# Router logits from the residual with scaled weights, and the tokens copied out by halves of the chunks

## The reference

```python
h = rmsnorm(x, lw['norm_ffn']) * (1 + scale2) + shift2
x = x + gate2 * moe_ffn(h, lw)

def moe_ffn(h, lw):
    scores = jax.nn.sigmoid((x @ lw['router_w']).astype(jnp.float32))   # x is h here, 256 tokens x 1024
    sel = scores + lw['router_bias'].astype(jnp.float32)
    ...                                    # the best 4 of 8 groups, in them the best 6 of 64 experts
    gates = gates / jnp.sum(gates, axis=-1, keepdims=True) * ROUTED_SCALE
    routed = moe_dispatch(x, eidx, gates, lw['exp_w_gate'], lw['exp_w_up'], lw['exp_w_down'])
    shared = swiglu(x, lw['sh_w_gate'], lw['sh_w_up'], lw['sh_w_down'])
    return (routed + shared).reshape(B, L, D)
```

## Time and profile before

| | us |
|---|---|
| median of 3 runs | 1344.55 |
| lowest and highest | 1344.04 and 1345.78 |
| the profiled execution, its own time | 1345.73 |
| its span | 1343.9 |
| mean granted TensorE clock | 0.967 |

### The profile page before, as it was taken

One profiled execution on the slowest core, in us unless ns is written; L12 is line 12 of the kernel. 1 busy time (PEld: TensorE's weight loads), 2 busy tenths in 40 slices (PEclk: granted clock), 3 DMA queues, 4 the chain that ended last, 5 costly groups with the idle time before them and its releaser, 6 DMA issues.

```text
span 1343.9 us, 22748 instructions
## 1 busy us (share of the span) xinstructions
PE 1235.8 (92%) x9612; PEld 838.9 (62%) x9612; DVE 273.3 (20%) x714; ACT 236.1 (18%) x521; POOL 2.8 (0%) x13
## 2 busy tenths in 40 slices
PE   6999999999998889888999999999999889888986
PEld 4566687667755566556565668866767565556554
DVE  1253342110111010101034424411011010101012
ACT  2363131110010001000134431311010001000102
POOL 0000000000000000000000000000000000000000
PEclk8999999999999899889999999999999899899989
DMA  9879849999999999999956663999999999999992
GB/s 385 323 316 346 348 190 410 383 422 420 420 420 422 422 422 422 422 422 422 402 201 264 244 242 152 415 383 422 422 420 421 421 421 422 422 422 422 422 419 85
DMA packets 80657, 496.58 MB, mean 369 GB/s; under 512 B 10576, under 2 KB 12880, under 8 KB 24784
## 3 DMA queue, kind: packets, MB, share of 16 engines
q1 hardware_dynamic: 76528, 493.63, 89.7%
q10 hardware_dynamic: 4064, 2.00, 0.5%
HBM read 493.60 MB, written 2.00 MB: 369 GB/s over the span
## 4 chain that ended last, share of the span: by engine, by line
PE 71%; DMA 23%; DVE 2%; issue 1%; SPq 1%; ACT 1%; DVEq 0%; ACTq 0%
DMA dn<-in_exp_w_down 19%; PE PS L2147 15%; PE PS L2183 13%; PE PS L2077 8%; PE PS L2084 7%; PE PS L1649 7%; PE PS L1981 4%; DMA gu<-in_exp_w_gate 3%; PE PS L1573 2%; PE PS L2043 2%; PE PS L1605 2%; DMA gu<-in_w_in 1%; PE PS L1772 1%; PE PS L1783 1%; PE PS L2123 1%
## 5 line engine op out<-in xcount | busy, mean ns | idle before, releaser
L2147 PE MATMUL PS<-gu,arena 128*32 128x256 f32 (+1 forms) x3072 | 316.6, 381 | 0.0
L2183 PE MATMUL PS<-arena 128*64 128x512 f32 (+1 forms) x336 | 177.9, 679 | 62.1 <-DMA dn<-in_exp_w_down 60.6
L2147 PEld LDWEIGHTS PS<-gu,arena 128*32 128x32 f32 (+1 forms) x3072 | 183.9, 118 | 79.0 <-issue 18.0
L2183 PE MATMUL PS<-dn,arena 128*32 128x512 f32 (+1 forms) x688 | 185.6, 637 | 0.0
L2077 PE MATMUL PS<-arena 128*128 128x128 f32 x1408 | 176.3, 278 | 0.5 <-ACT arena L1023 0.5
L2077 PEld LDWEIGHTS PS<-arena 128*128 128x128 f32 x1408 | 164.1, 192 | 17.9 <-issue 16.7
L2084 PE MATMUL PS<-arena 128*128 128x256 f32 x704 | 160.2, 380 | 1.4 <-ACT arena L1006 1.4
L2147 PE MATMUL PS<-arena 128*64 128x256 f32 (+1 forms) x672 | 152.0, 379 | 0.0
L2084 PEld LDWEIGHTS PS<-arena 128*128 128x128 f32 x704 | 130.2, 190 | 20.5 <-ACT arena L1006 3.2
L1484 DVE TENSOR_TENSOR arena<-arena,PS 128x256 f32<-128x256 f32 x44 | 18.5, 422 | 563.7 <-ACT arena L1019 563.7
L1006 ACT ACTIVATE arena<-PS 128x512 f32<-128x512 f32 x88 | 52.6, 597 | 459.0 <-PE PS L2183 459.0
(11 more groups left out here) (257 smaller groups left out, 1022.9 us busy)
## 6 DMA issues: line engine op xcount, KB each, us to landing
gu<-in_exp_w_gate SPq DMA_DIRECT2D x106, 1024.0 KB, 16.5
gu<-in_exp_w_up SPq DMA_DIRECT2D x86, 1024.0 KB, 17.6
dn<-in_exp_w_down SPq DMA_DIRECT2D x86, 1024.0 KB, 18.1
arena<-in_exp_w_up SPq DMA_DIRECT2D x42, 1024.0 KB, 14.9
arena<-in_exp_w_down SPq DMA_DIRECT2D x42, 1024.0 KB, 16.7
gu<-in_w_ada SPq DMA_DIRECT2D x20, 2048.0 KB, 8.8
xh<-in_exp_w_gate SPq DMA_DIRECT2D x22, 1024.0 KB, 11.3
gu<-in_w_in SPq DMA_DIRECT2D x8, 2048.0 KB, 13.1
```

The source lines that it names most:

```text
L2147: ins = mmul(PS[w * h:w * h + w, 5, FF * half:FF * half + FF], xg[:, k, w * h:w * h + w], weights[half][:, k], start=(k == 0), stop=(k == ...
L2183: ins = mmul(PS[w * h:w * h + w, 7 - n, :], hidT[:, j * P + w * h:j * P + w * h + w], weights[:, j, 512 * n:512 * n + 512], start=(j == 0) ...
```

## The change

The logits are no longer taken from `hT`. Since h = x * r * amp + shift, with r the inverse root of a token, `amp` and `shift` a number for each channel and group, the logits are r * (x @ (amp * W)) + shift @ W. So the product x @ (amp * W) can run on `xT` before r is there.

- **Weights.** In the last projection VectorE makes `scaled_rt` (two products 128x512, one for each group), `shift_rt` (two more) and `shift_sum` (the sum of `shift_rt` over the chunks). They wait for `router_in`. `amplify` for this norm moves from the end of the squares to before the copy of `kdec`.
- **TensorE in the norm.** The fills are gone. In their place stand one product that sums `shift_sum` over the partitions into bank 2 and the 16 products of the router, 8 before the sum of squares, 4 after it, 4 after the spread.
- **VectorE.** It copies the shift's logits out of bank 2, norms four chunks and modulates group 1 of three (`SECOND_D`), makes the logits (two instructions 128x64), and norms the other four.
- **ScalarE.** The table of the sigmoid is loaded by a 1-element call ahead of the first modulation. ScalarE modulates group 0 of chunks 0 to 2, takes the sigmoid of the logits, modulates both groups of chunks 3 to 5, copies out the tokens of chunks 0 to 3 (`tokens_out(l, 0)`), modulates chunks 6 and 7, and copies out chunks 4 to 7.
- **TensorE behind the norm.** It takes chunk by chunk: the two transposes, the shared gate's first half (chunks 0 to 6) and, for chunks 0 to 3, its second half. What was four products between `tallied` and `ranked` is one. The list of experts goes to bank 1 instead of 2.
- `h_d` counts fewer steps (`h_d_count`), also in SP's wait ahead of line 693. In layer 0's first norm a semaphore between two VectorE steps is replaced by another, and TensorE waits for the later of the two.

```diff
+        SECOND_D = 3
...
-                    A(hT[:, c, 0:P], xn[:, c, 0:P], ACT.Identity, scale=amp[:, w, c, 0:1],
-                      bias=mod[:, l, 3 * w, c, 0:1]).then_inc(S["h_a"], 1)
+                    for g in range(2 if k % 2 and c >= SECOND_D else 1):
+                        ins = A(hT[:, c, g * P:g * P + P], xn[:, c, g * P:g * P + P], ACT.Identity, scale=amp[:, w, c, g:g + 1],
+                                bias=mod[:, l, 3 * w, c, g:g + 1])
+                    ins.then_inc(S["h_a"], 1)
+                    if k % 2 and c == SECOND_D - 1:
+                        act.wait_ge(S["logits_ready"], l + 1)
+                        A(score, score, ACT.Sigmoid).then_inc(S["sig_exp"], 1)
+                    if k % 2 and c == 5:
+                        tokens_out(l, 0)
...
+                if k % 2:
+
+                    normed(0)
+                    for c in range(SECOND_D):
+                        normed(c + 1)
+                        modulated(c)
+                    v.wait_ge(S["router_done"], l + 1)
+                    for g in range(G):
+                        ins = stt(score[:, g], PS[:, 4, g * E:g * E + E], small[:, G + g:G + g + 1],
+                                  shift_sum[:, g * E:g * E + E], ALU.mult, ALU.add)
+                    ins.then_inc(S["logits_ready"], 1)
+                    for c in range(SECOND_D + 1, NC_):
+                        normed(c)
+                    return
...
+                def routed(cs):
+                    for c in cs:
+                        pe.wait_ge(S["x_bank"], x_steps(2 * l) + [c in step for step in STEPS[0]].index(True) + 1)
+                        for g in range(G):
+                            ins = mmul(PS[:, 4, g * E:g * E + E], xT[:, c, g * P:g * P + P], scaled_rt[:, g, c],
+                                       start=(c == 0 and g == 0), stop=(c == NC_ - 1), skip_group_check=True)
+                    return ins
+                pe.wait_ge(S["x_bank"], x_steps(2 * l) + 1)
+                pe.wait_ge(S["router_scaled"], l + 1)
+                mmul(PS[:, 2, 0:G * E], C("ones"), shift_sum, start=True, stop=True)
+                routed(range(4))
```

More of the change, by code:

```diff
@@ L810, in ada, with tokens_out @@
                 settle("ada_r")
+            def tokens_out(l, half):
+                act.wait_ge(S["t_h"], 2 * l + half + 1)
+                A(h_tok[:, :, 4 * half:4 * half + 4], PS[:, 2 * half:2 * half + 2, :].rearrange("p g (c t) -> p g c t", c=4), ACT.Copy
+                  ).then_inc(S["h_tok_a"], 1)
             def norm(k):
@@ L1349, in _ @@
                 ada(ADA_BY[l] - 1)
+                amplify(2 * l + 1)
                 v.wait_ge(S["t_k"], l + 1)
@@ L1354, in _ @@
                 v.tensor_copy(dk_tok, PS[:, 2, 256:512]).then_inc(S["ktok_ready"], 1)
+                v.wait_ge(S["router_in"], 16 * (l + 1))
+                router = w_rt.rearrange("p (c e) -> p c e", c=NC_)
+                for g in range(G):
+                    tt(scaled_rt[:, g], router, bc(amp[:, 1, :, g], 2, E), ALU.mult)
+                tt(shift_rt[:, 0], router, bc(mod[:, l, 3, :, 0], 2, E), ALU.mult)
                 v.wait_ge(S["t_mix"], 2 * l + 2)
@@ L1385, in _ @@
                         add_squares(STEPS[0][b - 1])
-                amplify(2 * l + 1)
                 add_squares(STEPS[0][-1], True)
@@ L1633, in norm @@
                 ins.then_inc(S["ss_ready"], 1)
-                fill(1)
-                pe.wait_ge(S["rstd_ready"], k // 2 + 1)
+                routed(range(4, 6))
+                pe.wait_ge(S["rstd_ready"], l + 1)
                 for g in range(G):
@@ L1640, in norm @@
                 ins.then_inc(S["rstd_spread"], 1)
-                fill(2)
+                routed(range(6, NC_)).then_inc(S["router_done"], 1)
             def project(bank, o, lhs, rhs, fresh=None):
@@ L2023, in _, with shared_part @@
                 norm(2 * l + 1)
[L2026 to L2046 removed]
+                w = piece(("shared", l, 0)).rearrange("p (u k t j) -> p u k j t", u=2, k=NC_, j=2)
+                def shared_part(bank, u, j, ks, first=None):
+                    for k in ks:
+                        ins = mmul(PS[:, bank, j * T:j * T + T], w[:, u, k, j], hT[:, k, :],
+                                   start=(k == 0 if first is None else first), stop=(k == NC_ - 1), skip_group_check=True)
+                    return ins
+                for c in range(NC_):
+                    pe.wait_ge(S["h_a"], NC_ * (2 * l + 1) + c + 1)
+                    pe.wait_ge(S["h_d"], h_d_count(2 * l + 1, c))
+                    for g in range(G):
+                        ins = turn(PS[:, 2 * (c // 4) + g, (c % 4) * P:(c % 4) * P + P], hT[:, c, g * P:g * P + P])
+                    if c % 4 == 3:
+                        ins.then_inc(S["t_h"], 1)
+                    if c < NC_ - 1:
+                        shared_part(6, 0, 0, (c,), first=(c == 0))
+                    if c < 4:
+                        shared_part(6, 0, 1, (c,), first=False)
                 pe.wait_ge(S["routed"], l + 1)
```

71 lines of the change are left out of this document (32 added, 39 removed).

## The result

The changed kernel takes 1338.29 us (median of 5; 1336.17 to 1340.38) where the kernel before, measured beside it, takes 1345.34 (median of 5): a ratio of 0.9949 [0.9936, 0.9963], 7.05 us faster. The forecast of 1340.2 with a range from 1339.0 to 1343.3 had the direction right, and the mechanism as far as TensorE's lead goes.

What follows compares the result with a forecast made beforehand. TensorE's work sets the first expert round, and its lead pays up to the transfer holes, 3.7 us in layer 0 and 2.0 in layer 1. Gains of 2.4 and 2.0 sum to 4.4: 1344.55 to 1340.2 us, range 1339.0 to 1343.3.

Steps and rivals of the forecast that it cites:

- Weights in the last projection, 0 us: VectorE's weight products and sum around the mixT copy: hidden in idle time, costing 0 us.
- Router in place of the fills, 0.3 us lost at the spread: TensorE in the norm: router records at 0.127 us each start the spread 0.3 us later, bounds 0 and 0.4.
- Logits and routing, 2.1 to 2.2 us earlier: VectorE in the norm: logits between the norms let the routing start 2.1 to 2.2 us earlier.
- ScalarE: ScalarE in the norm: table load fits by 0.2 us, modulations take 0.4 each, the count starts at most 1.1 late.
- TensorE 2.4 us ahead, bounds 1.5 and 2.7: TensorE behind the norm: list of experts and first expert round come 2.4 us earlier, bounds 1.5 and 2.7.
- Layer 0, 2.4 us: Transfers in layer 0: hole at 228 us closes, the big one shrinks to about 1.3; gain 2.4 us.
- Layer 1, capped at the hole of 2.0: Transfers in layer 1: the 2.0 us hole closes or nearly so; gain 2.0 us, bounds 1.3 and 2.4.
- A: ScalarE's queue holds the count, so the shift is 1.2 us in each layer: 1342.1 us; chance 0.14.
- B: Transfers hide the lead, holes closed by something else or refilled later, nothing left: 1344.5 us; chance 0.12.
- C: Slow weight products on VectorE before the mixT copy end the projection 4.4 us late per layer: 1348.9 us; chance 0.05.
- D: TensorE's clock falls to 1.2 GHz without fills, cutting the shift to 0.7 us per layer: 1343.1 us; chance 0.04.
- The gain above 5.5: Whole kernel: a gain above 5.5 us, if the holes give more than their lost bytes; chance 0.05.

Runs made afterwards that it cites:

- e1: Changed kernel with three unread 128x512 TensorE instructions just before the first expert round of each layer; 1344.2 us against 1344.59 for the kernel before (0.9991).
- e2: Changed kernel with three unread 128x512 TensorE instructions before the first expert round of layer 1 alone; 1340.25 us, 0.9971 of the kernel before.
- e10: Changed kernel with all eight second halves of the modulation back on VectorE, logits still behind three; 1342.56 us against 1344.06 for the kernel before (0.9992).
- e11: Changed kernel with one unread 128x512 TensorE instruction just before the first expert round of each layer; 1339.59 us in one run.
- e6: Changed kernel without the early call that loads the sigmoid's table; 1337.1 us against 1344.08 for the kernel before (0.9945).
- e8: Changed kernel with two chunks of the shared gate moved into TensorE's idle time ahead of the list of experts; 1335.51 us against 1344.08 before (0.9935).
- e12: Repeat of the changed kernel with two shared-gate chunks moved ahead of the list; 1335.92 us beside 1337.23 for the changed kernel (0.9940 of the kernel before).
- e7: Changed kernel with the third product of the router's weights repeated six more times on VectorE; 1341.43 us against 1344.08 for the kernel before (0.9979).
- e5: Kernel before without the norm's five filling instructions, nothing in their place; 1350.57 us against 1344.08 for the kernel before (1.0047).
- e16: Repeat of the changed kernel with six more products of the router's weights on VectorE; 1344.38 us in one run.
- after: The changed kernel itself in its first profile; its timed median is 1338.29 us against 1345.34 for the kernel before (0.9949).
- e9: Changed kernel, unchanged, timed and profiled again; 6.8 us faster than the kernel before (0.9946).
- e15: Changed kernel, unchanged, one more profile; 1337.19 us in one run.

## Why the prediction was off

**What bounds the kernel:** right. TensorE's stream sets the first round, and with a shorter lead more transfer time is lost and the layer takes longer (e1, e2, e10, e11). But the kernel is not bound by transfers to its end, and behind TensorE's last wait for one the gain goes on.

**Weights in the last projection, 0 us:** right. The sum over the chunks took 1.92 us and not 1.3; the idle time behind it was enough. The cover at the mixT copy is 2.8 us and not 2.1.

**Router in place of the fills, 0.3 us lost at the spread:** wrong, the spread starts 3.31 us behind the projection's end, for 3.46 before: 0.15 gained. I took 0.127 a record from a stretch that modulation paced; sixteen took 1.74 us to the next instruction, 0.109 each, the lower bound. That is 0.45 of the 0.5 us by which the lead was too small. The other terms of the lead are not measured one by one: five modulations are worth 1.28 us (e10), the table load 0.24 (e6), and by difference some 1.4 of the 2.9 are left for the router and the order behind it.

**Logits and routing, 2.1 to 2.2 us earlier:** 2.65, by the same 0.45; the steps between were right (2.1 us from the first norm to the logits, four norms in 1.40, the sigmoid in time).

**ScalarE:** right. The table load ends, the call with it, 0.2 us ahead of the first normed chunk, the modulations took 0.40 each, the last transposes came before the count was free. The count waited for VectorE.

**TensorE 2.4 us ahead, bounds 1.5 and 2.7:** 2.89, over the bound by the router's records.

**Layer 0, 2.4 us:** 2.3 came up to the last wait, so the number is right, in part by luck: the lead was 2.9 and not 2.4, and 1.7 us of hole are left where 1.3 were forecast. Another 0.7 lies behind the wait.

**Layer 1, capped at the hole of 2.0:** this is the step that failed, 4.7 us in the profiles. There is a cap, as e8 and e12 show, but it lies higher. The prediction reads one hole of 8 us and stops; the dip at 904 to 908, with all engines busy, belongs to it: it is in the profiles with the hole (e1) and gone with it. With its 0.9 us the loss there is about 3, the lost time of the whole stage fell from 3.6 to 1.0, and 3.4 us came up to the last wait. The other 1.4 us lie behind that wait and stood in no term, as the 0.7 of layer 0: the prediction puts all that follows the holes at nothing ("behind it the transfers never pause again"). The size rests on three profiles a kernel. The timed runs of e2, which take 2.5 of the 2.9 us of lead out of layer 1, give 1.7 to 2.7 us for it.

**Rivals:** A and B did not happen. C's mechanism exists (e7) from 2.8 us on. D's does too, closer to the kernel than I priced it. The gain above 5.5, at 0.05, is what came, and in part for the reason named there, that the holes give more than their counted bytes; it had deserved several times that chance, since the count left out every stretch at a share near 1.00.

## What to carry to other kernels

Where transfers bound a stage, sum the rate over the whole of it and not over the visible hole: the stretch behind a hole can be slow with every engine busy, and a lead on the engine that frees the buffers is worth about the sum, and nothing beyond it. Then look at what lies behind the last transfer, where other things set the time. Filling work that looks idle may be holding the clock; useful work can take its place, while an empty place cost more here than the filler. When a change has several parts, one that stands in its name may pay nothing: here it was the early copy of the tokens, and the five modulations moved to ScalarE paid. And before a difference is put down to a kernel, look at every place in the same profiles where it could show: the clock behind one wait looked like the kernel's own in layer 1 and varied by as much within one kernel in layer 0.

## What the runs showed of the hardware

Without the fills the granted clock fell to 1.2 GHz behind waits of 1.90 and 0.55 us and stayed there 13.7 us in layer 0 (e5, PEclk 0.50 from 190 to 202 us) and 10.2 in layer 1, most of them with TensorE fully busy; the distance grew by 4.8 and 3.6 us. Behind a wait of 1.6 us in one kernel it fell in one layer and held in the other (e10), and once it fell behind 0.99 us (e16). Behind the wait of 5.2 us it stayed low for 2.8, 3.9 and 5.4 us in three executions of one kernel (after, e9, e15, layer 0). The page "TensorE: Matmul & The Clock Gate" of the Trainium skill, section "What's actually happening", says that the point of change varies with the run, and these traces agree.

Behind a stretch in which the transfers stood partly still, the rate fell once more, to 328 GB/s over 4 us with the 16 engines 99% busy. Why, no run here asks.
